# Two-block kernel: output product begun on half its input, gate row made in the merge, router in plain float32

## What is computed

```python
merged = g_attn * (attn @ nsa_w_o) + g_ssm * (ssm @ ssm_w_o)
x = x + g1 * (merged @ w_out)                       # the output product
h = rms_norm(x, norm2_g) * (1.0 + sc2) + sh2
g_prob = softmax(h @ w_group + b_group)             # router: 4 groups,
e_logits = h @ w_expert + b_expert                  # 32 experts; 2 of a group are chosen
x = x + g2 * (weighted sum of the two experts' FFNs of h)
return rms_norm(x, final_g)
```

## Time and profile before

| | us |
|---|---|
| median of 3 runs (lowest, highest) | 1948.64 (1947.96, 1949.06) |
| the profiled execution | 1948.33 |
| its span (first to last instruction) | 1947.0 |
| lies around the span | 1.33 |
| PE busy, 9150 matmuls | 1728.9 (89%) |
| DVE busy | 950.2 (49%) |
| ACT busy | 713.5 (37%) |
| POOL busy | 260.1 (13%) |
| mean DMA rate | 129 GB/s |
| granted TensorE clock, share of 2.4 GHz | 0.93 |

### The profile page before, as it was taken

The page is one execution under the profiler, slowest core; times in us unless marked ns, Lnnn a source line. Parts: engine busy times, 40 slices in busy tenths (PEclk is TensorE's granted clock), DMA queues, the critical chain, the costliest instruction groups (busy, mean ns, idle before and its releaser), DMA issues. The chain is left out here.

```text
span 1947.0 us, 24155 instructions
## 1 busy us (share of the span) xinstructions
PE 1728.9 (89%) x9150; PEld 1307.7 (67%) x9150; DVE 950.2 (49%) x1877; ACT 713.5 (37%) x1583; POOL 260.1 (13%) x233
## 2 busy tenths in 40 slices
PE   4999969898999999979998999979998537999992
PEld 3887759777888888868887677768886423333330
DVE  3652464455766666563244766633534652222214
ACT  3432762244333334543221566653432201222111
POOL 1000025101222200000000011110101112333230
PEclk9999989989999999989976999989998857999996
DMA  6221000032444433413000000033106227999963
GB/s 241 110 89 44 1 1 2 32 147 82 181 196 196 199 134 122 156 61 138 36 22 1 7 7 7 7 139 143 44 1 247 99 87 282 369 393 388 377 238 145
DMA packets 39937, 251.67 MB, mean 129 GB/s; under 512 B 17744, under 2 KB 17744, under 8 KB 23312
## 3 DMA queue, kind: packets, MB, share of 16 engines
q1 hardware_dynamic: 23120, 223.49, 29.3%
q10 hardware_dynamic: 2880, 15.07, 2.0%
q0 software_dynamic: 13824, 11.58, 1.9%
HBM read 293.99 MB, written 18.87 MB: 161 GB/s over the span
## 5 line engine op out<-in xcount | busy, mean ns | idle before, releaser
L600 ACT ACTIVATE units<-arena 128x512 fp32r<-128x512 f32 (+2 forms) x435 | 261.4, 625 | 502.9 <-PE banks L2227 499.8
L1195 DVE TENSOR_TENSOR units<-arena,units 128x512 fp32r<-128x512 f32 x388 | 259.7, 694 | 323.3 <-ACT units L600 322.8
L2225 PE MATMUL banks<-hx,units 128*128 128x512 f32 x800 | 313.6, 392 | 6.6 <-DVE units L1195 4.2
L2227 PE MATMUL banks<-hx,units 128*128 128x512 f32 x800 | 311.5, 389 | 0.0
L2226 PE MATMUL banks<-hx,units 128*128 128x512 f32 x800 | 311.4, 389 | 0.0
L600 ACT ACTIVATE arena<-banks 128x512 f32<-128x512 f32 (+3 forms) x230 | 130.5, 571 | 283.8 <-PE banks L2149 97.7
L2149 PE MATMUL banks<-arena 128*128 128x128 f32 (+3 forms) x704 | 116.8, 305 | 88.5 <-POOL arena L1993 40.7
L2225 PE MATMUL banks<-units 128*128 128x512 f32 x416 | 165.5, 398 | 14.8 <-DVE units L1195 14.8
L2225 PEld LDWEIGHTS banks<-hx,units 128*128 128x128 f32 x800 | 150.3, 188 | 38.9 <-issue 4.5
L2149 PEld LDWEIGHTS banks<-arena 128*128 128x128 f32 (+3 forms) x704 | 90.6, 162 | 122.4 <-issue 82.6
L2227 PEld LDWEIGHTS banks<-hx,units 128*128 128x128 f32 x800 | 150.3, 188 | 31.6
(11 more groups left out here) (404 smaller groups left out, 2534.3 us busy)
## 6 DMA issues: line engine op xcount, KB each, us to landing
arena<-in_moe_gu SPq DMA_DIRECT2D x32, 2048.0 KB
arena<-in_w_in SPq DMA_DIRECT2D x17, 2048.0 KB
arena<-in_moe_dn SPq DMA_DIRECT2D x32, 1024.0 KB, 9.7
arena<-in_ada SPq DMA_DIRECT2D x12, 2048.0 KB
arena<-in_w_gu SPq DMA_DIRECT2D x11, 2048.0 KB
arena<-in_w_out SPq DMA_DIRECT2D x4, 2048.0 KB
arena<-in_w_down SPq DMA_DIRECT2D x4, 2048.0 KB
arena<-in_cmp_w SPq DMA_DIRECT2D x2, 2048.0 KB
```

The source lines that it names most:

```text
L600: return func(dst, src, ACT.Copy, scale=scale)
L1195: tt(U[:, u % 4, 1, :], src, U[:, u % 4, 0, :].bitcast(F32), SUB).then_inc(*up("gemm_dve", "lo", c.part, u))
L2225: pe.matmul(bs[i], sh[:, q], mh, start=c.first and k == 0, stop=False)
L2227: ins = pe.matmul(bs[i], sl[:, q], mh, start=False, stop=c.last and k == c.kn - 1)
```

## The change

1. **g1 row at the start of the merge.** DVE makes the diagonals in two operations of 128x512, PE multiplies ones by them in two matmuls of 512 columns, ACT copies both banks to `grow`, between steps 2 and 3 of `glu`. In the same place DVE prepares the router: `wr_b` = router weights times the shift, its column sums by PE (8 matmuls) plus the bias are the constant row `wr_c`; the router weights are multiplied by `sc2` in place.
2. **Output product begun on half its input.** The two `w_out2` chunks have no `ready` wait any more. ACT waits for `mT[k]` step by step, so steps 0 to 3 need only the half c = 0. The items of `ssm_wo1` move between steps 2 to 5 of `w_out20`. The loads go to slots 2 and 3 (`self.turn = 2`); the `moe` loads follow at slots 0, 1, 2, 3. The DMA of `x4` is issued by ACT behind step 6 of `w_out20`, and DVE waits for it behind step 1 of `w_out21`.
3. **Gate in the weights.** DVE multiplies the 8 weight tiles of `w_out21` by the second half of the row, one behind each step of `w_out20`; the items of `w_out21` lose their multiplication.
4. **Norm begun early, no fences.** The squares of the first column half are taken by ACT during `w_out21`, those of the second right behind its items. The tables for the square root and the exponential are called in ahead by small operations.
5. **Router on unscaled rows.** The rows of `x4`, not `xs5`, are transposed and multiplied by the router weights as plain float32, 32 matmuls of 36 columns; the first column half during `w_out21` (transposes ahead of its steps 4 to 7, two of the four groups of products ahead of steps 6 and 7). DVE then multiplies the logits by the reciprocal norm and adds `wr_c`.
6. **Moved**: the scaled rows `xs5` are made by ACT alone, during the route, behind its first exponential; behind them ACT copies the g2 row. SP writes `xs5` after that, and waits for the write to land before the first `moe_dn` loads. POOL clears the gather buffers as soon as `w_out21` is done.

The core of the diff:

```diff
@@ Plan
+        self.turn = 2
         for n in range(2):
             self.load(f"w_out2{n}", I["w_out2"][n])
...
-            self.add(Chunk(f"w_out2{n}", f"w_out2{n}", w8(r(f"w_out2{n}")), 8, "late", True, m.mT,
-                           (("gemm_pool", "mT", 1, 3),)))
-        self.narrow("wr", "late")
+            self.add(Chunk(f"w_out2{n}", f"w_out2{n}", w8(r(f"w_out2{n}")), 8, "late", True, m.mT))
@@ act_program.gemm
         for k in range(c.kn):
+            if name == "w_out21":
+                a.wait_ge(*at("gemm_dve", "gained", k))
             hi_of(c, k, "w", c.w[:, k, :])
+            if name.startswith("w_out2"):
+                a.wait_ge(*at("gemm_pool", "mT", k // 4, k % 4))
@@ act_program
+    def between(k):
+        if k == 6:
+            a.wait_ge(*at("gemm_dve", "ms", 1, 3))
+            a.dma_start(m.x4, m.xb_d.rearrange("(t p) d -> p t d", p=128)).then_inc(*up("dma_x4", by=16))
+    gemm("w_out20", "ssm_wo1", between)
+    func(m.rs_tmp[:, 63:64], ones1, ACT.Sqrt)
+    def between(k):
+        if 3 <= k < 7:
+            a.wait_ge(*at("gemm_dve", "add", "w_out20", k - 3))
+            square("n2", 0, 0, k - 3, m.x4)
+        if k >= 5:
+            router_T(0, k - 5)
+    gemm("w_out21", "w_out20", between)
+    router_T(0, 3)
+    for t in range(4):
+        a.wait_ge(*at("gemm_dve", "add", "w_out21", t))
+        square("n2", 0, 1, t, m.x4)
+        if t in (1, 3):
+            router_T(1, t - 1)
+    root("n2", m.r4, m.rs_tmp[:, 0:4])
+    func(m.rs_tmp[:, 63:64], ones1, ACT.Exp)
     a.wait_ge(*at("route", "gsub"))
     func(m.ge, m.ge, ACT.Exp).then_inc(*up("route_act", "gexp"))
+    for t in range(4):
+        copy(m.xs5[:, t, :], m.x4[:, t, :], m.r4[:, t:t + 1]).then_inc(*up("norm_act", "scaled", "n2", t))
+    for half in range(2):
+        row_of("g2", half)
     a.wait_ge(*at("route", "esub"))
@@ dve_program
+    def between(k):
+        c = p.chunks["w_out21"]
+        if k == 0:
+            v.wait_ge(*at(f"ring{p.ring[c.load][0]}", c.load))
+        tt(c.w[:, k, :], c.w[:, k, :], m.grow[:, 512:1024], MUL).then_inc(*up("gemm_dve", "gained", k))
+    gemm("w_out20", "ssm_wo1", between)
+    def between(k):
+        if k == 1:
+            v.wait_ge(*at("dma_x4"))
+        if k >= 6:
+            row_of("g2", m.mod[:, 40:48], m.diag2, k - 6)
+    gemm("w_out21", "w_out20", between)
+    for i in range(4):
+        item("w_out21", i)
+        if i == 2:
+            router_T(1)
+    router_T(3)
...
+    v.wait_ge(*at("rx_pe", "logits"))
+    tt(m.lg, s.bank("logits")[:, 0:144].rearrange("p (t n) -> p t n", t=4), bc(m.r4.unsqueeze(2), 4, 36),
+       MUL).then_inc(*up("rx_dve", "logits"))
+    v.wait_ge(*at("rx_dve", "logits"))
+    tt(m.lg, m.lg, bc(m.wr_c.unsqueeze(1), 4, 36), ADD).then_inc(*up("rx_dve", "lg"))
     dve_route(v, m, s)
@@ pe_program
+    def router_T(h, t, engine):
+        b = take(("rx", h, t), (engine, "xt", h, t), among=free[0:3])
+        pe.wait_ge(*at("gemm_dve", "add", f"w_out2{h}", t))
+        for f in range(4):
+            ins = tp(b[:, H4[f]], m.x4[:, t, H128(4 * h + f)])
+        ins.then_inc(*up("rx_pe", "xt", h, t))
+    def router(h, t, engine):
...
+        pe.wait_ge(*at(engine, "xt", h, t))
+        for f in range(4):
+            ins = pe.matmul(b[:, 36 * t:36 * t + 36], m.x4T[h][t][:, H4[f]], C["wr"][:, 4 * h + f, :],
+                            start=h == t == f == 0, stop=h == 1 and t == f == 3)
+    def ahead(k):
+        if k >= 6:
+            router(0, k - 6, "rx_act")
+        if k >= 4:
+            router_T(0, k - 4, "rx_act")
+    gemm("w_out21", None, ahead)
+    router(0, 2, "rx_act")
+    router(0, 3, "rx_act")
+    engine = ("rx_act", "rx_dve", "rx_act", "rx_dve")
+    for t in range(5):
+        if t < 4:
+            router_T(1, t, engine[t])
+        if t:
+            ins = router(1, t - 1, engine[t - 1])
@@ sp_program.load
-                sp.wait_ge(*at("norm_dve", "scaled", "n2", 2))
-                sp.wait_ge(*at("norm_pool", "scaled", "n2", 3))
+                sp.wait_ge(*at("norm_act", "scaled", "n2", 3))
                 sp.dma_start(m.xs_d.rearrange("(t p) d -> p t d", p=128), m.xs5).then_inc(*up("dma_xs", by=16))
-                fence(18)
+                sp.wait_ge(*at("dma_xs"))
                 for i in range(4):
                     down(i)
```

More of the change, by code:

```diff
@@ L372, in merge_views @@
         self.x4 = self.at(xo, 4, 1024)
[L373 to L379, removed]
+        o = self.o_att + 8192
+        self.diag1, self.wr_b = self.at(o, 1024), self.at(o + 1024, 8, 36)
+        self.top = o + 512
+        self.lg, self.wr_c = self.new(4, 36), self.new(36)
+        self.x4T = [[self.at(p + 2048 * h + 512 * t, 512) for t in range(4)] for h in range(2)]
+        self.xs5 = self.at(self.o_att, 4, 1024)
     def moe_views(self):
@@ L1028, in act_program @@
     for c, name in enumerate(MERGE):
[L1029 to L1041, removed]
-    fence(18)
+        def between(k):
+            if c == 0 and k >= 2:
+                row_of("g1", k - 2)
+        gemm(name, MERGE[c - 1] if c else None, between)
+    def between(k):
[19 more added lines that the diff above has]
+    func(m.rs_tmp[:, 63:64], ones1, ACT.Exp)
     a.wait_ge(*at("route", "gsub"))
     func(m.ge, m.ge, ACT.Exp).then_inc(*up("route_act", "gexp"))
+    for t in range(4):
+        copy(m.xs5[:, t, :], m.x4[:, t, :], m.r4[:, t:t + 1]).then_inc(*up("norm_act", "scaled", "n2", t))
+    for half in range(2):
+        row_of("g2", half)
     a.wait_ge(*at("route", "esub"))
@@ L1795, in dve_program @@
     fence(16)
+    for half in range(2):
+        row_of("g1", m.mod[:, 16:24], m.diag1, half)
+    tt(m.wr_b, C["wr"], bc(m.mod[:, 24:32].unsqueeze(2), 8, 36), MUL).then_inc(*up("row_dve", "wr_b"))
+    tt(C["wr"], C["wr"], bc(m.sc2.unsqueeze(2), 8, 36), MUL).then_inc(*up("rx_dve", "wr"))
     for c, name in enumerate(MERGE):
         gemm(name, MERGE[c - 1] if c else None)
[L1798 to L1801 removed]
@@ L2363, in first_X, with row_of @@
         ins.then_inc(*up("gdn_pe", "X", t))
-    def row_of(key, tmps):
-        take(("row", key, 0), ("row_act", key, 0), hold=True)
-        take(("row", key, 1), ("row_dve", key, 1), hold=True)
-        for f in range(8):
-            pe.wait_ge(*at("row_dve", key, "diag", f))
-            b = s.bank_now("row", key, f // 4)
-            pe.matmul(b[:, H4[f % 4]], ones, tmps[f % 2], start=True, stop=True).then_inc(*up("row_pe", key, f))
-        drop(("row", key, 0))
-        drop(("row", key, 1))
+    def row_of(key, diag):
+        for half in range(2):
+            b = take(("row", key, half), ("row_act", key, half))
+            pe.wait_ge(*at("row_dve", key, half))
+            pe.matmul(b, ones, diag[:, 512 * half:512 * half + 512], start=True, stop=True).then_inc(*up("row_pe", key, half))
     def values(v, n):
@@ L2588, in pe_program @@
     fence(16)
+    row_of("g1", m.diag1)
+    b = take(("wr_c",), ("row_dve", "wr_c"))
+    pe.wait_ge(*at("row_dve", "wr_b"))
+    group(b[:, 0:36], [(ones, m.wr_b[:, f, :]) for f in range(8)]).then_inc(*up("row_pe", "wr_c"))
     for name in MERGE:
-        gemm(name, ("n1", False, "mid"))
-    row_of("g1", m.row_tmp1)
+        gemm(name, ("n1", "mid"))
     gemm("w_out20")
-    gemm("w_out21")
-    fence(17)
-    to_hx("n2", m.xs5, True)
-    row_of("g2", m.row_tmp2)
-    narrow("wr", 36, m.wr_tmp, ("n2", True, "mid"))
-    fence(18)
+    free = tuple(s.place["w_out20", i] for i in range(4))
+    def router_T(h, t, engine):
[5 more added lines that the diff above has]
+    def router(h, t, engine):
+        if h == 0 and t == 0:
+            take(("logits",), ("rx_dve", "logits"), hold=True, among=free[3:4])
+        b = s.bank_now("logits")
+        pe.wait_ge(*at(engine, "xt", h, t))
+        for f in range(4):
+            ins = pe.matmul(b[:, 36 * t:36 * t + 36], m.x4T[h][t][:, H4[f]], C["wr"][:, 4 * h + f, :],
+                            start=h == t == f == 0, stop=h == 1 and t == f == 3)
+        return ins
+    def ahead(k):
[12 more added lines that the diff above has]
+            ins = router(1, t - 1, engine[t - 1])
+    ins.then_inc(*up("rx_pe", "logits"))
+    drop(("logits",))
+    row_of("g2", m.diag2)
     b = take(("route", "pos"), ("route", "cnt"))
```

140 lines of the change are left out of this document (52 added, 88 removed).

## The result

| | before | after |
|---|---|---|
| median of the runs | 1948.61 us (4 runs, 1947.96 to 1949.06) | 1899.76 us (4 runs, 1898.09 to 1902.83) |
| profiled execution (span) | 1948.33 (1947.0) | 1902.83 (1901.5) |

The ratio is 0.9751, 95% interval 0.9734 to 0.9768. Five more runs of the changed kernel beside nine of the kernel before gave 0.9754 (0.974 to 0.9768). Forecast were 1897.4 us, within 1891.5 to 1904.

A forecast was written before the change was run, and what follows sets the result against it. Chains handed between engines were taken to bound the gap before the output product, norm and router, and route; PE the product, PE and DMAs the experts' stage. 11.1 + 38.5 + 1.3 = 50.9 us off 1948.33 gave 1897.4, within 1891.5 to 1904.

The forecast's parts named there:

- Sum: Whole kernel: 11.1 + 38.5 + 1.3 = 50.9 us won from 1948.33, giving 1897.4 us.
- Part 1: Merge's end to output product's end: PE goes on without a gap on half the input, 11.1 us won.
- POOL's hit: Output product: POOL's additions slow DVE operations beside them, 0.43 at each of four steps, taken as 1.5 us of stall.
- The rival that had them strung up: In `w_out20` DVE and POOL run one after the other: stall of 6 us, total 1901.9; chance 0.13.
- Router products: Output product: 8 small float32 matmuls ahead of each of two steps add 0.9 us.
- Late `x4`: Output product: the load of `x4` meets `moe2` and lands after DVE asks, 1.0 us; bounds 0 and 10.
- its rival (21 us again): Output product: `x4` takes 21 us to land as before, 9 us more, total 1906.4; chance 0.08.
- Part 2: Norm and router, product's end to route's first operation: 47.1 us become 8.6, 38.5 us won; bounds 7.5 and 11.
- a cold PE: Norm and router: small matmuls at 1.2 GHz would add some 1.7 us; 8.6 taken against 7.8 at full clock.
- Part 3: Route: it starts with the exponential's table in place, 1.3 us won, no drain counted.
- Covers: Merge's start: g1 row and router constants hide in the wait for `glu`, 0 us; 4 if that cover is gone.
- the rival with all covers: No stall (2.5 less), warm PE in the tail (0.8), warm merge start (2): total 1892.1 us; chance 0.12.

The follow-up runs named there:

- DVE adds: Changed kernel with the second half's four additions on DVE, not POOL, and weight multiplications two each behind steps 0, 1, 6, 7; 1896.92 us, 0.9736 of the kernel before.
- no preload: Changed kernel without the small exponential that calls the table in ahead; 1897.79 us, route 33.64 us against 33.65.
- the last variant of scaled rows: Changed kernel with the router on scaled rows behind the product, plus seven unread matmuls that keep PE busy; 1902.80 us, norm and router 17.99 us.

## Why the prediction was right, and where it wasn't

- **Sum.** 50.9 us were forecast for the three stages, 50.2 measured. The chains that were to go did go, but the closeness is partly luck: in parts 1 and 2 errors of opposite sign nearly cancel, and part 3 came out for another reason than the one given.
- **Part 1: 11.1 forecast, 10.15 measured.** No gap and no cold start, as forecast. The variants take the 49.96 apart: 192 matmuls 43.5; transposes and router products 3.6 (49.96 less 46.37); POOL beside DVE 2.8 (49.96 less 47.16); nothing is left for `x4`. Forecast were 1.9 + 0.9 = 2.8, then 1.5, and 1.0. Three terms were mis-sized; the first two came to 2.1 us too little, and the third gave 1.0 of it back:
  - *POOL's hit*, 1.5. I took one hit of 0.43 for each step, where the pair of two waits for POOL's end. DVE's round grew by 3.51 - 2.72 = 0.79 us at each of four steps, 3.2 in all, of which 2.8 reached PE. The rival that had them strung up had the mechanism right and priced it at 6, too high. The Trainium skill (SBUF — State Buffer, Who interferes with whom) tells of an exclusive lock between a DVE instruction with two SBUF inputs and a GpSimd one that reads SBUF. The trace agrees: about the whole 1.29 us pair lies behind POOL's end, L1816 keeps its 0.68 us beside a POOL that only writes, and the items, which read one operand from a PSUM bank, ran beside POOL's additions unslowed already before (four in 2.48, beside four additions in 4.92).
  - *Router products*, 0.9. "28 small matmuls took 6.15" was misread: a plain float32 matmul leaves two records, so x28 are 14. Four products are 8 records and take 0.81 us at full clock (1514.51 to 1515.32), 1.6 for the two steps.
  - *Late `x4`*, 1.0, and its rival (21 us again). I had `moe2` start 2.5 us behind it with 1.1 MB through; its bytes began some 6.3 us behind, with 1.77 through, so the 0.45 to 2.31 of the earlier trace rows never came into play. How the two queues share when they do meet was not tested here. In DVE adds, without the stall, `x4` lands at 1483.46 + 7.8 = 1491.3 and DVE asks at 1493.5: still in time.
- **Part 2: 38.5 forecast, 38.41 measured**, by two errors that cancel, so by luck. I had 7.8 us at full clock and took 0.8 more for a cold PE; the clock was 1.00. But the last transposes end at 1527.84 + 0.64 = 1528.48, 5.7 us in, where I had 4.5, since the products ahead of them cost twice what I took (the misreading of part 1 again). PE's work did not end inside DVE's chain, as I had it, but set its pace: PE is busy for 8.43 of the 8.68 us, and DVE waits 1.80 us for the last transposes; the copy, root and logits follow as forecast, each about 1 us later than listed.
- **Part 3: 1.3 forecast, 1.62 measured**, and the reason given fell. The load is out of the route (no preload shows it), but not through the preload. The Trainium skill (ScalarE: Activation LUTs, What ACT_TABLE_LOAD costs) adds a drain of 1380 ns to the load. Here the activation follows the load at 1529.74 + 1.28 within 0.01 us, and 1.62 is all that the route won, not 2.7; on this point the measurement decides. Of the other 0.3, 0.27 lies in one DVE operation of the route that took 0.45 us before, at 1576.92, and 0.18 now. The second exponential comes at 1538.68, 7.2 us into the route where it was 8.9; ACT's copies end 0.41 us ahead of it, so they just fit, as forecast, and the first gather moved with it.
- **Covers.** The g1 row and the router's constants in the merge's start cost nothing: ACT waits 1.49 us for `glu` there, where it waited 1.52, and PE starts 2.1 us behind ACT's first split (1305.63 to 1307.74), where it started 2.2 behind. No warm start came of it either, so the rival with all covers lost that part. The experts' stage kept its clock of 0.94.
- **The rest of the difference.** The median is 2.4 us above the forecast. 0.7 of that lies in the three stages, the rest in the others. PE's clock rises there at different moments. The same window of PE's first work, in the kernel before, the changed kernel and the last variant of scaled rows (the third number from the end is the clock):

```profile
32.00:40.00 8.00, 7.57 (x34) 6.30 (x34) 3.37 (x6) 1.86 (x4) 0.00 (x0) 1.00 0.00 0
```

```profile
32.00:40.00 8.00, 7.49 (x21) 5.98 (x22) 2.75 (x5) 1.34 (x3) 0.00 (x0) 0.60 0.00 0
```

```profile
32.00:40.00 8.00, 7.37 (x32) 6.12 (x33) 3.57 (x6) 2.01 (x4) 0.00 (x0) 1.00 0.00 0
```

In both of the first two PE had done its first 32 matmuls (5.58 and 5.88 us of work) by 32.00. The second then does 21 where the first does 34: 13 x 0.2267, 3 us, are lost at once. Over the twelve profiles with the changed start the merge began between 1303.48 and 1308.59 us, mean 1306.1, and the experts' stage took 324.9 to 328.0, mean 326.4 against before's 326.49. Whether the mean start, 1.9 us later than the one profile of before, is chance or a trace of the change (constants loaded at the start) the profiles can't say, since there is only that one of before. The times say a little more: the nine runs of the changed kernel average 1900.4 us, the thirteen of the kernel before beside them 1948.4, 48.0 apart, with a standard error of some 0.8. If the three stages won 50.2 in each of them, about 2 us were lost elsewhere, more than chance would easily give. What loses them stays open.

What stays argued only: that it is POOL's reading, and not the addition's length, that holds the pair up; that the lock is taken per instruction; and what the compiler goes by when it places a table load.

## What to carry to other kernels

Look for work that a product can do on the half of its input that is ready, and move the loads with it: here each of the two without the other gave 2.0 to 2.4 of 10 us. Postpone a scaling that a long chain must wait for (a norm's factor) until behind the product that is linear in it: of 14.3 us, 9 were the clock that PE lost while it waited. And don't put an addition of two SBUF operands on POOL beside a nearly full DVE: POOL's four cost 2.8 us, and DVE made them itself for nothing once other work had been moved off these steps.

## What the runs showed of the hardware that was not expected

- Seven matmuls that nobody reads, in a 6.3 us pause of PE, took 9.05 us off the tail: behind the pause PE ran at 1.2 GHz for all of 20.7 us without them, and at 2.4 GHz with them. The kernel with the filling did 18.0 us of tail where the one without did 27.0.
- DVE and POOL with SBUF operands on both sides ran one after the other: pair 1.29 to 2.38 us, POOL's addition 1.23 to 1.67. DVE operations with one operand in a PSUM bank ran beside the same additions at 0.62 us each, unslowed.
- The load of an activation table can be placed ahead of a wait that the program has in front of the activation: 1526.08, 3 us before the values came.
- A load of 2 MB issued by SP at 1492.83 had moved nothing by 1495, more than 2 us later; until then ACT's queue had the DMA engines to itself.
- Kernels with the same code up to there reached the merge's first matmul at times up to 5.1 us apart. 3 us of such a difference arose in one stretch of 8 us, where PE's clock was 0.60 instead of 1.00.
